# Routing of a mixture layer: experts by rank, the first pair's rows fetched on their own, and unread matmuls in TensorE's waits

## The reference

```python
gl = (x @ w_group) + b_group                  # 4 groups
top_g = argmax(gl); p_g = softmax(gl)[top_g]
el = ((x @ w_router) + b_router).reshape(T, 4, 4)
top_v, top_i = top_k(el[top_g], 2)            # 2 of the 4 experts of that group
p_e = softmax(top_v) * p_g
...
y += (silu(x @ w_gate[e]) * (x @ w_up[e]) * gate[e]) @ w_down[e]   # for each of 16 experts e
```

## Time and profile before

| | us |
|---|---|
| median of 3 runs | 693.25 (692.15 to 695.26) |
| profiled execution | 694.91 |
| its span, first to last instruction | 693.2 |
| TensorE busy | 636.0 (92%) |
| VectorE busy | 205.7 (30%) |
| ScalarE busy | 143.5 (21%) |
| GpSimd busy | 30.0 (4%) |
| mean granted TensorE clock | 0.954 of full |

### The profile page before, as it was taken

How to read it: one execution, slowest core, us unless ns; L and a number is a source line. 1 busy time by engine, 2 the same in 40 slices (tenths; PEclk the granted TensorE clock), 3 DMA queues, 4 the chain that set the end, 5 groups by cost and what they waited for, 6 DMA issues and landing times.

```text
span 693.2 us, 7668 instructions
## 1 busy us (share of the span) xinstructions
PE 636.0 (92%) x2933; PEld 391.7 (57%) x2933; DVE 205.7 (30%) x602; ACT 143.5 (21%) x396; POOL 30.0 (4%) x56
## 2 busy tenths in 40 slices
PE   6889999999958899999988999999997589999994
PEld 3567877777644444555446777777765334344431
DVE  2233011222045143444444333333312611212311
ACT  1112012322041011111032333333212301111110
POOL 4000000000002000000001000000000300000000
PEclk9999899999985999999999999999999589999998
DMA  9996132213333669999996505131334358999921
GB/s 288 274 276 215 61 126 85 95 61 121 122 125 122 273 282 413 420 423 418 360 348 225 183 1 182 38 147 61 121 122 152 129 210 333 408 422 420 420 113 62
DMA packets 59113, 150.03 MB, mean 216 GB/s; under 512 B 10082, under 2 KB 42914, under 8 KB 46786
## 3 DMA queue, kind: packets, MB, share of 16 engines
q1 hardware_dynamic: 55554, 136.71, 53.4%
q0 software_dynamic: 2912, 10.64, 4.5%
q10 hardware_dynamic: 608, 2.16, 0.8%
HBM read 146.27 MB, written 3.23 MB: 216 GB/s over the span
## 4 chain that ended last, share of the span: by engine, by line
PE 83%; DMA 6%; DVE 5%; ACT 2%; issue 2%; SPq 1%; ACTq 0%; DVEq 0%
PE bank L1169 34%; PE bank L1387 15%; PE bank L1411 7%; DMA ring<-in_moe_w_up 6%; PE bank L1426 3%; PE bank L1430 3%; PE bank L1264 3%; PE bank L1369 2%; PE bank L1178 1%; PE bank L1548 1%; PE bank L1535 1%; PE bank L1356 1%; PE bank L1196 1%; PE bank L1577 1%; PE bank L1300 1%
## 5 line engine op out<-in xcount | busy, mean ns | idle before, releaser
L1169 PE MATMUL bank<-xT,ring 128*128 128x272 f32 x640 | 158.4, 404 | 5.2 <-ACT qk_area L518 3.0
L1169 PEld LDWEIGHTS bank<-xT,ring 128*128 128x128 f32 x640 | 123.6, 196 | 32.9 <-issue 6.4
L1387 PE MATMUL bank<-ring,gate_area 128*64 128x512 f32 x512 | 119.7, 622 | 7.6 <-ACT gate_area L617 2.6
L1387 PEld LDWEIGHTS bank<-ring,gate_area 128*64 128x64 f32 x512 | 39.8, 143 | 81.5 <-issue 81.5
L1169 PE MATMUL bank<-tok,ring 128*128 128x272 f32 (+1 forms) x256 | 61.0, 391 | 0.6 <-DVE tok L1153 0.6
L1411 PE MATMUL bank<-ring,gate_area 128*64 128x512 f32 x256 | 57.9, 593 | 0.0
L1169 PEld LDWEIGHTS bank<-tok,ring 128*128 128x128 f32 x256 | 47.4, 190 | 13.5 <-issue 6.1
L929 DVE TENSOR_TENSOR qk_area<-qk_area,bank 128x256 f32<-128x256 f32 x16 | 6.7, 418 | 114.6 <-ACT qk_area L625 114.6
L1411 PEld LDWEIGHTS bank<-ring,gate_area 128*64 128x64 f32 x256 | 19.5, 137 | 35.3 <-issue 35.3
L451 POOL DMA_INDIRECT qk_area<-xs,idx x16 | 17.9, 1117 | 463.6 <-DVE idx L815 339.4
L1426 PE MATMUL bank<-big 128*128 128x272 f32 x128 | 32.5, 399 | 1.2 <-DVE big L943 1.2
(11 more groups left out here) (243 smaller groups left out, 573.4 us busy)
## 6 DMA issues: line engine op xcount, KB each, us to landing
ring<-in_moe_w_gate SPq DMA_DIRECT2D x32, 1024.0 KB, 12.3
ring<-in_moe_w_up SPq DMA_DIRECT2D x32, 1024.0 KB, 13.7
ring<-in_moe_w_down SPq DMA_DIRECT2D x32, 1024.0 KB, 7.5
ring<-in_m_w_in SPq DMA_DIRECT2D x12, 1024.0 KB, 11.8
ring<-in_kv_w SPq DMA_DIRECT2D x8, 1024.0 KB, 12.0
ring<-in_m_w_out SPq DMA_DIRECT2D x4, 1024.0 KB, 9.0
ring<-in_f_w_q SPq DMA_DIRECT2D x4, 1024.0 KB, 12.5
ring<-in_f_w_o SPq DMA_DIRECT2D x4, 1024.0 KB, 5.2
```

The source lines that it names most:

```text
L1169: ins = pe.matmul(bank[c % 2][:, 0:n], w[:, k, half * P:half * P + P], x[:, k, 0:n], start=(k == 0), stop=(k == KB - 1))
L1387: ins = pe.matmul(bank[1][s, :], xgT[b % 2][:, q, s], ring[:, r:r + 2, q * FE:(q + 1) * FE], start=(q == 0), stop=(q == KB - 1))
```

## The change

- *Rank in place of maxima.* For the group logits and each group of four expert logits (one 5 x 4 row for a token, `fives`), all pairs are compared at once: `bt` is each value less each other one, compared with `tie`, which is -1e-37 where the other one comes first and 0 elsewhere; the sum gives the number of values that beat each (`rank`). The group is the one with rank 0, the mask of chosen experts is rank below 2 in that group, and `e12` is rank 0 and rank 1.
- *Positions.* The bases of all four blocks (`base4`) come in one matmul ahead of the mask; the sums add to it.
- *First pair alone.* `one_hot` covers only the first 128 slots before the first slot matmuls; row numbers of pair 0 are written at once, and its gather waits for them and for the rows written. One-hots of pairs 1 to 3 follow on VectorE, with the two weights of a token behind them; their slot matmuls (18 in layer 0, 12 in layer 1) stand behind the transposes of pair 0, in `bank[1]`, and one write makes the numbers of pairs 1 to 3. The one-hots of pairs 4 to 7 stand behind those.
- *Moved behind `gate_up(0)`:* the four spreading matmuls and their copies, `combine_weights(0)` and `(1)`, and the sums for further rounds.
- *ScalarE* writes all rows first, its two exponentials follow.
- *Unread matmuls.* `keep_busy(n)` issues n float32 matmuls of 128 x 128 on 128 columns into a part of `bank[3]` that nothing reads: 3 (layer 0) or 6 (layer 1) ahead of the mask, 8 behind the positions, 18 behind the first slot matmuls.

The diff, without most of its unchanged lines and its declarations:

```diff
...
-        elg = sb("elg", [P, 3, EPG])
-        o12 = sb("o12", [P, 2, 3, EPG])
+        rank = rt[:, 348:408].rearrange("p (t g e) -> p t g e", t=3, g=NG + 1)
+        beats = colT[0][:, 0:240]
...
+            const(pool.affine_select(out=tie[:, :, :], in_=tie[:, :, :], compare_op=ALU.is_ge, fill=-1e-37, base=0,
+                                     pattern=[[-1, EPG], [1, EPG]], channel_multiplier=0))
...
-            const(pool.tensor_scalar(rev[:, :], iota_f[:, 0:EPG], -1.0, float(EPG), ALU.mult, ALU.add))
-            const(pool.tensor_scalar(base16[:, :], iota_f[:, 0:NE], float(CAP), None, ALU.mult))
+            for t in range(3):
+                const(pool.tensor_scalar(base4[:, t, :], iota_f[:, 0:NE], float(CAP), None, ALU.mult))
...
-                    pool.wait_ge(*in_layer("idx_ready", l, min(b // 2, 2) + 1))
+                    pool.wait_ge(*in_layer("idx_ready", l, (1, 2, 2, 2, 3)[min(b, 4)]))
...
-                rows_out(*tiles[0][:2])
-                act.wait_ge(*in_layer("gl_sub", l, 1))
-                act.activation(t4b[:, 0:nt, :], t4[:, 0:nt, :], ACT.Exp).then_inc(sem("gl_exp"), 1)
-                rows_out(*tiles[1][:2])
-                if l == 0:
-                    rows_out(*tiles[2][:2])
-                act.wait_ge(*in_layer("v_sub", l, 1))
-                act.activation(ex[:, 0:nt, :], dv[:, 0:nt, :], ACT.Exp).then_inc(sem("v_exp"), 1)
+                for t, rows, _ in tiles:
+                    rows_out(t, rows)
...
+                act.wait_ge(*in_layer("gl_sub", l, 1))
+                act.activation(t4b[:, 0:nt, :], t4[:, 0:nt, :], ACT.Exp).then_inc(sem("gl_exp"), 1)
+                act.wait_ge(*in_layer("v_sub", l, 1))
+                act.activation(ex[:, 0:nt, :], dv[:, 0:nt, :], ACT.Exp).then_inc(sem("v_exp"), 1)
...
-                for r in range(4):
-                    act.wait_ge(*in_layer("bc_mm", l, r + 1))
-                    act.activation(bc4[:, r, 0:n], bank[4 + r][:, 0:n], ACT.Copy).then_inc(sem("bc_ready"), 1)
+                def rows_spread():
+                    for r in range(4):
+                        act.wait_ge(*in_layer("bc_mm", l, r + 1))
+                        act.activation(bc4[:, r, 0:n], bank[4 + r][:, 0:n], ACT.Copy).then_inc(sem("bc_ready"), 1)
...
+                    else:
+                        rows_spread()
...
-                revb = rev[:, :].unsqueeze(1).to_broadcast(bc3)
-                gl, el = lg[:, 0:nt, 0:NG], groups(lg[:, 0:nt, NG:NG + NE])
-                t4n, t4bn, dnn, elgn, gmn, pgn, exn, dvn = [a[:, 0:nt, :] for a in (t4, t4b, dn, elg, gm, pg, ex, dv)]
+                gl, el = lg[:, 0:nt, 0:NG], lg[:, 0:nt, NG:NG + NE]
+                t4n, t4bn, dnn, gmn, pgn, exn, dvn = [a[:, 0:nt, :] for a in (t4, t4b, dn, gm, pg, ex, dv)]
...
-                def first_max(dst, src, mx):
-                    link(dve.tensor_tensor(t4n, src, mx.to_broadcast(bc3), ALU.is_equal))
-                    link(dve.tensor_tensor(t4n, t4n, revb, ALU.mult))
-                    link(dve.tensor_reduce(dnn, t4n, AX.X, ALU.max))
-                    link(dve.tensor_tensor(dst, t4n, dnn.to_broadcast(bc3), ALU.is_equal))
+                n5 = nt * (NG + 1)
+                fives = rt[:, 288:288 + n5 * EPG].rearrange("p (g e) -> p g e", e=EPG)
+                each = [P, n5, EPG, EPG]
+                bt = beats[:, 0:n5 * EPG * EPG].rearrange("p (g e j) -> p g e j", e=EPG, j=EPG)
+                rk5 = rt[:, 348:348 + n5 * EPG].rearrange("p (g e) -> p g e", e=EPG)
+                rk = rank[:, 0:nt, 1:NG + 1, :]
...
+                ins.then_inc(sem("lg_read"), 1)
+                dve.wait_ge(*in_layer("lg_read", l, 1))
+                link(dve.tensor_tensor(bt, fives.unsqueeze(2).to_broadcast(each), fives.unsqueeze(3).to_broadcast(each),
+                                       ALU.subtract))
+                link(dve.tensor_tensor(bt, bt, tie[:, :, :].unsqueeze(1).to_broadcast(each), ALU.is_gt))
+                link(dve.tensor_reduce(rk5, bt, AX.X, ALU.add))
+                link(dve.tensor_scalar(og[:, 0:nt, :], rank[:, 0:nt, 0, :], 0.0, None, ALU.is_equal))
+                dve.scalar_tensor_tensor(groups(eall[:, 0:nt, :]), rk, 2.0, ogb, ALU.is_lt, ALU.mult) \
+                    .then_inc(sem("eall_ready"), 1)
+                for c in (0, 1):
+                    ins = dve.scalar_tensor_tensor(groups(e12[:, c, 0:nt, :]), rk, float(c), ogb, ALU.is_equal, ALU.mult)
...
-                link(dve.tensor_reduce(gmn, gl, AX.X, ALU.max))
-                first_max(og[:, 0:nt, :], gl, gmn)
-                dve.tensor_tensor(t4n, gl, gmn.to_broadcast(bc3), ALU.subtract).then_inc(sem("gl_sub"), 1)
-                t16v = groups(t16[:, 0, 0:nt, :])
-                link(dve.tensor_tensor(t16v, el, ogb, ALU.mult))
-                link(dve.tensor_reduce(elgn, t16v.rearrange("p t g j -> p t j g"), AX.X, ALU.add))
-                dve.wait_ge(*in_layer("gl_exp", l, 1))
-                dve.tensor_reduce(pgn, t4bn, AX.X, ALU.add)
-                link(dve.tensor_reduce(v12[:, 0, 0:nt, :], elgn, AX.X, ALU.max))
-                first_max(o12[:, 0, 0:nt, :], elgn, v12[:, 0, 0:nt, :])
-                link(dve.scalar_tensor_tensor(elgn, o12[:, 0, 0:nt, :], NEG, elgn, ALU.mult, ALU.add))
-                link(dve.tensor_reduce(v12[:, 1, 0:nt, :], elgn, AX.X, ALU.max))
-                first_max(o12[:, 1, 0:nt, :], elgn, v12[:, 1, 0:nt, :])
-                dve.tensor_tensor(dvn, v12[:, 1, 0:nt, :], v12[:, 0, 0:nt, :], ALU.subtract) \
-                    .then_inc(sem("v_sub"), 1)
-                for c in (0, 1):
-                    ins = dve.tensor_tensor(groups(e12[:, c, 0:nt, :]), ogb,
-                                            o12[:, c, 0:nt, :].unsqueeze(2).to_broadcast(full), ALU.mult)
-                link(ins)
-                dve.tensor_tensor(eall[:, 0:nt, :], e12[:, 0, 0:nt, :], e12[:, 1, 0:nt, :], ALU.add) \
-                    .then_inc(sem("eall_ready"), 1)
-                link(dve.reciprocal(pgn, pgn))
+                def one_hot(c0, base, w):
+                    for c in (0, 1):
+                        for t, rows, _ in tiles:
+                            ins = dve.tensor_scalar(sel[0:rows, c, t, c0:c0 + w], iota_f[0:rows, 0:w], float(base),
+                                                    tok4[0:rows, c, t:t + 1], ALU.add, ALU.is_equal)
+                    ins.then_inc(sem("sel_ready"), 1)
...
-                for c in (0, 1):
-                    ins = dve.tensor_tensor(t16[:, c, 0:nt, :], slots[:, 0:nt, :], e12[:, c, 0:nt, :], ALU.mult)
-                link(ins)
+                both = [P, 2, nt, NE]
+                link(dve.tensor_tensor(t16[:, :, 0:nt, :], slots[:, 0:nt, :].unsqueeze(1).to_broadcast(both),
+                                       e12[:, :, 0:nt, :], ALU.mult))
...
-                def one_hot(c0, base):
-                    for c in (0, 1):
-                        for t, rows, _ in tiles:
-                            ins = dve.tensor_scalar(sel[0:rows, c, t, c0:c0 + 256], iota_f[0:rows, :], float(base),
-                                                    tok4[0:rows, c, t:t + 1], ALU.add, ALU.is_equal)
-                    ins.then_inc(sem("sel_ready"), 1)
-                one_hot(0, 0)
-                one_hot(256, 256)
-                row_of_slot(l, 0, 0, 2, 1)
+                one_hot(0, 0, P)
+                link(dve.tensor_reduce(gmn, gl, AX.X, ALU.max))
+                dve.tensor_tensor(t4n, gl, gmn.to_broadcast(bc3), ALU.subtract).then_inc(sem("gl_sub"), 1)
+                link(dve.tensor_tensor(t16[:, :, 0:nt, :], el.unsqueeze(1).to_broadcast(both), e12[:, :, 0:nt, :], ALU.mult))
+                row_of_slot(l, 0, 0, 1, 1)
+                link(dve.tensor_reduce(v12[:, :, 0:nt, 0], t16[:, :, 0:nt, :], AX.X, ALU.add))
+                dve.tensor_tensor(dvn, v12[:, 1, 0:nt, :], v12[:, 0, 0:nt, :], ALU.subtract).then_inc(sem("v_sub"), 1)
+                one_hot(P, P, 2 * P)
+                one_hot(3 * P, 3 * P, P)
+                dve.wait_ge(*in_layer("gl_exp", l, 1))
+                link(dve.tensor_reduce(pgn, t4bn, AX.X, ALU.add))
+                link(dve.reciprocal(pgn, pgn))
...
-                row_of_slot(l, 1, 2, 4, 2)
-                dve.wait_ge(*in_layer("row4_mm", l, 1))
-                dve.tensor_copy(row4[:, 0:n], bank[3][0:MH, 0:n]).then_inc(sem("row4_ready"), 1)
-                one_hot(0, 512)
-                one_hot(256, 768)
...
+                def one_hot_late(c0, base):
+                    for c in (0, 1):
+                        for t, rows, _ in tiles:
+                            ins = dve.tensor_scalar(sel[0:rows, c, t, c0:c0 + 256], iota_f[0:rows, :], float(base),
+                                                    tok4[0:rows, c, t:t + 1], ALU.add, ALU.is_equal)
+                    ins.then_inc(sem("sel_ready"), 1)
...
+                def further_rounds():
+                    dve.wait_ge(*in_layer("idx_ready", l, 3))
```

(73 more changed lines are left out.)

## The result

| | before | after |
|---|---|---|
| median, same chip (12 runs each) | 693.42 us (691.92 to 696.30) | 688.62 us (687.13 to 692.37) |
| profiled execution, span | 694.91, 693.2 us | 687.83, 686.1 us |
| mean granted clock | 0.954 | 0.972 |

The ratio is 0.9931, 95% interval 0.9915 to 0.9947: faster by 4.8 us, for 4.95 forecast (688.3). The two profiled executions lie 7.1 us apart. 2.5 of that arose before the routing of layer 0, in code that the change doesn't touch: the clock fell once at 22.4 us in the one and not in the other. So I measure each stage from its layer's own logits.

What follows compares the result with a forecast made beforehand. Bound: two routing stretches (21.4, 18.8 us) of VectorE, a gather, then two rounds of transposes. Sum 9.2 - 1.45 - 1.3 + 0 - 1.5 = 4.95 us: 690.0 profiled, 688.3 median; range 681.5 to 692.5.

Steps and rivals of the forecast that it cites:

- The three steps of 240 elements: VectorE, layer 0 routing: two passes over 240 elements and a sum, 0.41 us taken for each.
- the 0.65 taken: VectorE, layer 0: 0.65 us lost to TensorE's six slot matmuls, which the second six one-hots used to hide.
- the positions: Layer 0: 9 matmuls in place of 12 hold VectorE about 1.05 us for 1.34, saving 0.3.
- What is late next: First gather waits for the rows written to memory, not for row numbers; starts 4.5 and 3.4 us earlier.
- Gather under one-hots: GpSimd writes the first gather's descriptors during VectorE's later one-hots: 0.3 us charged per layer, bounds 0 and 1.6.
- gather late: Rival: first gather's descriptors wait for one-hots (1.6 us per layer) or writes land later; gain 2.3, 691 us; chance 0.13.
- The clock: TensorE's clock falls again before pair 0's gate and up, in 5.7 and 5.5 us after the 18 unread matmuls.
- Gain 0: Pair 0's gate and up cost their 9 to 10 us as before: gain 0, bounds 4.9 and -2.
- Behind the first gate and up: The four spreading matmuls, moved there, lose 1.45 us in layer 0 and 1.3 in layer 1; bounds 1.0 and 3.5.
- The second gate and up: In layer 1 its hole grows from 4.3 to 5.6 us: 1.5 us charged, bounds 0 and 3.
- the first pair's lead: Pair 0's one-hots and row numbers first on VectorE; with ranks, row numbers come 4.7 and 3.9 us earlier.

Runs made afterwards that it cites:

- the last run: Changed kernel with the spreading matmuls back ahead of pair 0's transposes, plus 3 more unread matmuls between the two transposing rounds: 682.77 us, ratio 0.9848.
- the kernel with the one-hots ahead: Changed kernel with VectorE writing the one-hots of pairs 1 to 3 before pair 0's row numbers, not after: 693.75 us, ratio 1.0008.

## Why the prediction was right

**VectorE.** The three steps of 240 elements took 0.41, 0.41, 0.40, as taken. Of a one-hot 128 wide I took 0.15 and it is 0.21 (1.25 for six): near the 0.21 that 48 elements cost in the earlier trace rows, the row that I should have used. That made 0.35, and TensorE's slot matmuls held VectorE 0.1 longer than the 0.65 taken. What made it up was the positions: from the mask's end VectorE was held 0.80 us for 1.42, where I had counted 0.3 saved. So the numbers came 4.6 us earlier for 4.7, with two terms off against each other.

**What is late next.** In both layers the gather waits for the written rows, as forecast, and starts 4.6 and 3.8 us earlier for 4.5 and 3.4.

**Gather under one-hots.** Charged 0.3, bounds 0 and 1.6. From its start to the first transpose it is 4.74 and 4.65 us, less than the 4.9 forecast; GpSimd's span is 1.22 and 1.08. The rival "gather late" fell. The Trainium skill ("SBUF — State Buffer", "SBUF: two separate sides") has a VectorE instruction in a two-port mode keep GpSimd out of its descriptors for the whole of that instruction. These traces don't show which mode a one-hot runs in. This gather doesn't agree with a long wait: its 1.22 under one-hots is what the first gather of the kernel before took ahead of them (1.22). But others were slow: the second gather of layer 1, under one-hots too, took 2.65 us, as the earlier trace rows had it (2.62), though nothing waited for it, and layer 0's first gather took 1.84 in the last run, where VectorE's one-hots around it are the same. What decides is not shown.

**The clock.** The unread matmuls hold it until they end and through the gather, and it falls before gate and up, as forecast (in layer 1 already in the transposes). For gate and up they were put at 0, and it gained 0.7 and 1.3 us by the balance; the run without them puts all that they give at 3.5 (692.10 for 688.62; 2.4 by the ratios), as without them the transposes too run at the low clock (1.12 us a round for 0.71 in layer 0). From the last of the 18 to gate and up it was 5.8 and 6.05 us, for 5.7 and 5.5 forecast. "Gain 0" was measured against the kernel before, whose spreading hid at the low clock under the gather.

**Behind the first gate and up.** The hole grew by 2.03 us in layer 0 for 1.45: the clock fell in it, and the second round of transposes took 1.12 for 0.71. The second gate and up lost 2.88 in layer 1 for 1.5. These two terms (-1.96) and the first gate and up (+2.05) were both mis-sized, and cancel to 0.1. That the sum came within 0.2 us of the forecast is luck; that VectorE's steps bring the gain, that the writes are then late, and that the clock falls before gate and up is not.

**The shares.** The prediction gave ranks and the first pair's lead one term. The runs split it. Ranks alone give 4.6 us. Fetching the first pair on its own, with the spreading moved for it, loses 2.8 without unread matmuls (689.33 to 692.10; 2.2 by the ratios, whose intervals overlap, so this loss is not clear of noise) and gains 4.6 with them (693.20 to 688.62; 4.3 by the ratios; the number of unread matmuls differs too). The unread matmuls lose 3.9 us in the old order and win 3.5 (2.4) in the new one. The likely reason, which no run isolates, is when they start: in the new order the 18 follow 0.5 us behind the first slot matmul, at the full clock; in the old one the eight ahead of the transposes came 5 us after the clock had fallen. Experiments with both orders and one number of matmuls would be needed to part the two further.

Left open: 1.3 to 2.3 of the 5.1 us of the kernel with the one-hots ahead; and why three more matmuls held the clock in layer 1 and not in layer 0 of the last run.

## What to carry to other kernels

Unread matmuls paid where they started at TensorE's full clock and ended as the awaited data landed; behind a fall they ran at half speed and became the path (0.47 us each, 3.9 us in all). Shorten the single-file chain first: the ranks alone gave 4.6 us here, the other two parts together nothing that can be told until their order was mended. A piece moved from under a transfer to behind the matmuls that it delayed is not hidden there; put it where TensorE waits for a copy-out (that alone took 5.1 us off the kernel after, 4.2 by the ratios).

## What the runs showed of the chip that was not expected

A float32 matmul of 128 x 128 on 128 columns costs 0.238 us back to back at the full clock (18 in 4.29) and 0.47 at the low one. TensorE can be 100% busy and stay low: the four-row spreading (3.99 us for 2.10, in layer 0 of four kernels: before, ranks alone, and both with unread matmuls in the old order). Before routing, in code that no edit touched, the clock falls twice (from 22 and from 39 us) in five of the thirteen traces, once (from 36 to 38) in six, and not at all up to 48 us in two. Layer 0's logits follow it: 198.3 to 198.6 us in the five, 195.6 to 196.4 in the six, 194.5 and 194.7 in the two. The runs of one kernel lie 3 to 10 us apart, so two profiled executions must be compared stage by stage.
